# Letting a stage's row gathers be paced by free ring slots alone, without their wait for streamed dense tiles

## What is computed

```
def block(xb):                       # 128 tokens
    ...                              # top-k over product keys -> eidx, gate g
    u = u_tab[eidx]
    act = gelu(einsum('td,thkd->thk', xb, u))
    return einsum('thk,thkd->td', g * act, v_tab[eidx])
```

## Time and profile before

| | |
|---|---|
| median of 3 runs | 2384.32 us (2382.76 to 2390.59) |
| the profiled execution | 2381.75 us, of which the trace spans 2379.9 us |
| PE busy in the span | 2116.2 us |
| DVE busy | 1310.4 us |
| POOL busy | 892.9 us |
| data moved by DMA | 590.03 MB |
| gathers (queue q0) | 402.70 MB, 44.4% of 16 engines' span |

### The profile page before, as it was taken

How to read it: one execution, slowest core, us unless ns; L and a number is a source line. 1 busy time by engine, 2 the same in 40 slices (tenths; PEclk the granted TensorE clock), 3 DMA queues, 4 the chain that set the end, 5 groups by cost and what they waited for, 6 DMA issues and landing times.

```text
span 2379.9 us, 31321 instructions
## 1 busy us (share of the span) xinstructions
PE 2116.2 (89%) x12505; PEld 1569.1 (66%) x12505; DVE 1310.4 (55%) x2926; ACT 642.7 (27%) x1077; POOL 892.9 (38%) x821
## 2 busy tenths in 40 slices
PE   8999999999999998999999887889898887875775
PEld 8776879889887875888888654577785444311111
DVE  5855476776456466659798765689663233100000
ACT  4345332322454333331111143521111443100000
POOL 0500000000000000004577566557677665666664
PEclk9999999999999998999999998899999898897998
DMA  5111254444212210227999998989999998999997
GB/s 199 54 36 71 89 186 177 177 177 160 92 69 106 71 54 18 89 84 276 356 417 417 387 339 329 331 310 418 419 418 418 370 346 321 368 378 370 358 381 279
DMA packets 147057, 590.03 MB, mean 248 GB/s; under 512 B 16336, under 2 KB 16464, under 8 KB 134240
## 3 DMA queue, kind: packets, MB, share of 16 engines
q0 software_dynamic: 110592, 402.70, 44.4%
q1 hardware_dynamic: 35136, 178.80, 19.8%
q10 hardware_dynamic: 1184, 6.53, 0.7%
HBM read 584.29 MB, written 3.67 MB: 247 GB/s over the span
## 4 chain that ended last, share of the span: by engine, by line
PE 30%; DVE 13%; POOL 8%; issue 7%; DMA 6%; another core or an unknown queue 4%; ACT 3%; DVEq 0%; POOLq 0%; ACTq 0%
PE ps L1166 8%; DVE cols L1996 6%; POOL big L2687 5%; PE ps L1116 5%; PE ps L561 4%; PE ps L562 4%; PE ps L563 4%; DMA big<-vtab,big 2%; DMA big<-utab,cols 2%; PE ps L1103 2%; POOL hres L2687 2%; ACT Ir L2546 1%; PE ps L1130 1%; ACT Ir L2548 1%
## 5 line engine op out<-in xcount | busy, mean ns | idle before, releaser
L1103 PE MATMUL ps<-rowb,raw 128*128 128x256 f32 x2048 | 458.4, 384 | 23.6 <-DMA raw<-ucols 18.3
L1103 PEld LDWEIGHTS ps<-rowb,raw 128*128 128x128 f32 x2048 | 388.2, 192 | 90.5 <-issue 22.2
L1166 PE MATMUL ps<-big,cols 128*32 128x512 f32 x1392 | 362.7, 674 | 55.0 <-issue 32.0
L2687 POOL DMA_INDIRECT big<-vtab,big x348 | 338.6, 973 | 188.9 <-issue 84.0
L2611 POOL TENSOR_TENSOR small<-small,cols 128x1 f32<-128x1 f32 (+3 forms) x33 | 28.7, 872 | 886.1 <-DVE small L1612 387.4
L1166 PEld LDWEIGHTS ps<-big,cols 128*32 128x32 f32 x1392 | 70.4, 118 | 235.3 <-issue 149.2
L2687 POOL DMA_INDIRECT big<-utab,cols x139 | 177.7, 1278 | 86.3 <-issue 34.7
L1996 DVE CUSTOM_DVE_ANT_0 cols<-big 128x1024 bf16<-128x1024 f32 x139 | 167.9, 1226 | 40.4 <-DMA big<-utab,cols 27.5
L1116 PE MATMUL ps<-Aj,Ir 128*128 128x64 f32 x1024 | 159.0, 296 | 32.4 <-issue 23.9
L1166 PE MATMUL ps<-hres,cols 128*32 128x512 f32 x392 | 170.0, 666 | 18.8 <-issue 12.4
L2049 DVE TENSOR_TENSOR cols<-cols,ps 128x512 f32<-128x512 f32 x64 | 43.9, 688 | 246.3 <-PE ps L1116 138.8
(11 more groups left out here) (390 smaller groups left out, 4502.1 us busy)
## 6 DMA issues: line engine op xcount, KB each, us to landing
raw<-ucols SPq DMA_DIRECT2D x128, 512.0 KB
raw<-ff SPq DMA_DIRECT2D x32, 1024.0 KB, 5.0
raw<-w SPq DMA_DIRECT2D x24, 1024.0 KB, 4.8
raw<-ada SPq DMA_DIRECT2D x24, 1024.0 KB, 4.8
raw<-wo SPq DMA_DIRECT2D x8, 1024.0 KB, 4.8
raw<-wq SPq DMA_DIRECT2D x8, 1024.0 KB, 4.8
big<-vtab,big POOLq DMA_INDIRECT x348
hres<-x SPq DMA_DIRECT2D x8, 512.0 KB, 6.0
```

Of the source, the lines that this page charges most:

```text
L1103: ins = e.matmul(PS[b][:, c:c + 256], lhsT=un[j % NU][:, k, :], rhs=h2T[k // 4][:, k % 4, :], start=(k == 0), stop=(k == 7))
L1166: ins = e.matmul(PS[hf][32 * j:32 * j + 32, :], lhsT=win[:, c0:c0 + 32], rhs=gs[i][:, hf * 512:(hf + 1) * 512], start=(m == 0), stop=(m == ...
L2687: e.indirect_dma_start(gs[i], None, utab if st == "U" else vtab, bass.IndirectOffsetOnAxis(ap=idx, axis=0)).then_inc(sems[f"l_g{i}"], 16)
```

## The change

POOL's wait for the dense tiles in U1 is removed, and the constant with it. Nothing else changes: the same instructions, the same order on every engine, the same slots.

```
-BEHIND = 8
...
                     if st == "U":
                         G.wait_ge(*at[decoded(t, k)])
-                        if t and k >= BEHIND:
-                            for what, a, z in pace("U", t, k - BEHIND):
-                                if what == "dense" and z > a:
-                                    G.wait_ge(*at["dn", z - 1])
                         gather(st, t, k, eid[:, t, k:k + 1])
```

## The result

The changed kernel took 2422.88 us (median of 4 runs, 2399.24 to 2442.62), the kernel before 2383.54 us (4 runs, 2377.14 to 2390.59). The ratio is 1.0132, with a 95% interval of 1.0097 to 1.0168. The profiled execution took 2424.70 us, 42.95 more than that of before. Lines of the changed kernel stand two lower: gathers L2685, dots L1994, tiles' matmuls L1101, SP's tile loads L2742. ("L" numbers of experiments can be off by a few again.)

The account below looks back on a forecast made before the run. Full DMA engines at 418 GB/s were taken to bound U1. The profiled 2381.75 us, + 0 for tiles, - 0 for gathers, plus 2.57 us to the median, rounded to 2384 us; range of 8 in 10: 2375 to 2396 us.

Parts of the forecast that it names:

- U1 is as long as its bytes: In U1 the DMA engines are full, so its bytes set its length: 96.5 MB, 231 us at 418 GB/s.
- the sum of 184 pieces: U1's transfers from 1575 us: 122 gathers, 60 tile loads, write-out and read-back, 96.5 MB, through by 1806 us.
- The stall moves from `dn` to `dot`: In U1 POOL would wait for DVE's dots to free slots instead of PE's tiles; value 0.
- about 32 us in flight: A U1 gather's time in flight would grow from 19.34 us, with POOL up to 17 gathers ahead of DVE.
- The tiles lose nothing further; price 0: U1's tile loads would not slow when more gathers are queued; 0 us added.
- an even split: SP's tile queue and POOL's gather queue share bandwidth equally: 213 GB/s for tiles, which need 148.
- the far bound of +35: Upper cost from U1's beginning: 0.80 us of PE's wait per tile over 52 tiles, 42 us, less 7.
- U0, which I chose for its length: U0's 140 us without the wait, tiles 3.73 us each against 3.60 in U1: +1 us, taken as 0.
- Rival (b): Gathers crowd out U1's tile loads, which then finish last: +14, 2398 us; chance 0.16, spread from +7 to +35.
- (a): Rival: POOL's waits make U1's gathers late, so removal gains at most 7.02 us, 2377 us; over 0.3% faster has 0.09.
- (c): Rival: SP's write-out round trip in U1 takes longer behind more gathers, up to +3 us; no chance of its own.

Follow-up runs that it names:

- e7: The changed kernel as it is, run again where the kernel before took 2284.43 us; 2284.47 us, ratio 0.9996.
- e6: The changed kernel with POOL, from U1's gather 10 on, waiting for DVE's dot k - 10; 2383.51 us, 0.9997 of the kernel before.
- e13: The kernel before with its wait for the tiles loosened from step k - 8 to k - 16; 2385.71 us, ratio 1.0017.
- e14: The changed kernel with POOL at most 13 gathers ahead of DVE's dots in U1; 2381.18 us, 0.9992 of the kernel before.
- kind B: Groups of runs in which the kernel before takes about 2384 us, as in the recorded pair.
- kind A: Groups of runs in which the kernel before takes about 2284 us.
- e5: The changed kernel as it is, run again where the kernel before took 2385.18 us; 2395.39 us, ratio 1.0036.
- e11: The changed kernel as it is, run again where the kernel before took 2383.38 us; 2393.61 us, ratio 1.0033.
- e12: The changed kernel with SP's write-out of block 0 and read-back moved behind the last tile; 2379.18 us, 0.9982 of the kernel before.
- e1: The changed kernel with POOL at most 10 gathers ahead of DVE's dots in U1; 2285.83 us, 1.0001 of the kernel before.
- e10: The kernel before with its wait for the tiles loosened from step k - 8 to k - 16; 2284.27 us, ratio 1.0001.
- e15: The changed kernel with a small POOL power, in a new buffer, behind every second gather of U1; 2312.10 us, 1.0120 of the kernel before.
- e17: The changed kernel with a small POOL power, in a new buffer, behind every third gather of U1; 2301.91 us, 1.0080 of the kernel before.
- e18: The changed kernel with a small POOL power, in a new buffer, behind every fourth gather of U1; 2301.12 us, 1.0072 of the kernel before.

## Why the prediction was wrong, step by step

**"U1 is as long as its bytes"**: right, as long as gathers last. e7 took away all of POOL's waits for tiles and gained nothing (0.9996); with late marks absent, U1 kept 418 or 419 GB/s. In the changed kernel's recorded execution the rate holds too, until 1810 us, when the gathers have run out; from there the sum of 184 pieces no longer gives the time.

**"The stall moves from `dn` to `dot`", "about 32 us in flight"**: right. POOL waits for L1994 and no longer for PE; e7's gather was 31.25 us in flight. (17 gathers at 1.78 us are 30, not 32; the nearness of 31.25 to both decides nothing.) In the recorded execution the wait is short because the tiles' trouble left the bandwidth to the gathers.

**"The tiles lose nothing further; price 0"**: this is the step that failed. Its stated reason, an even split that does not depend on the other queue's length, held: 6.5 us from a tile load's issue to its landing with up to 13 gathers in flight, 6.7 in e7 with 14 to 16. What I had assumed without a row was the link ahead of it, that PE finishes a landed tile and its mark moves SP at once. In the recorded execution eight loads were issued 5.7 to 34.7 us late, and the term put at 0 came out at 43 us for the profiled launch. The profile of before had a trace of it that I did not look for: its load of tile 68 is issued 4.1 us after the end of tile 65, right behind POOL's free burst at U1's start, and I put the 2.57 us that PE then waited down to bandwidth. I even used them for the far bound of +35. If the rate of POOL's issues is what matters, which the count suggests and nothing shows, that stretch was the nearest thing to the changed kernel, and not U0, which I chose for its length.

**Rival (b)**: its picture came true, its mechanism did not. Named signs were a wait for `ucols` of 30 us or more (33.3), tile 123 behind the last dot (1857.5 against 1784.5) and a window well under 418 GB/s (163). But no tile load was crowded out. Its price, +14 with a far bound of +35, fell short of the +39 between the medians (+43 between the profiled executions), since I spread a small delay over 52 tiles, where most of it fell on eight.

**Why nothing stopped it** is my reading of the windows, argued and not tried by itself: with the gate, POOL waits for the same late tile, and the tiles find their bandwidth later with gathers still beside them. Without it the gathers go on at 420 GB/s, get up to 73 us ahead (1857.5 - 1784.5), and what is left at the end is tiles alone, one for each 3.45 us of PE's time, at 163 GB/s. The byte sum then no longer holds: half of the engines' time in those 47 us is lost. e6 (a cap of 10 to the dots, 0.9997) and e13 (`BEHIND = 16`, 1.0017) showed no runaway in 20 runs; e14 did in 2 of 11. At that frequency ten runs without one prove little for any single variant.

**(a)** did not happen anywhere: no variant's ratio is below 1 by more than its interval. **(c)** is small: from the write-out's issue to the read-back it is 8.66 us in the recorded execution, 8.66 in e7 and 8.59 before.

**What stays open.** Why marks of PE move SP and ACT late, and PE's matmuls come singly, in kind B only, and whether PE works late there or finished marks are held up. Small doses stand in every profile of kind B; why they become a runaway in some executions is open too. That it goes with gathers issued back to back is a count over eight profiles, not an experiment; the experiments meant for it met kind A, without the fault. Why the recorded four runs are so much slower (1.0132) than the fifteen of e5 and e11 (1.0036, 1.0033) is open as well; both hold long executions of the same sort (up to 2414.89), only fewer. No version was clearly faster than the kernel before: e12, the changed kernel with its write-out moved, comes closest in kind B (0.9982 [0.9963, 1.0001]) and is 0.9992 and 0.9999 in kind A.

## What to carry to other kernels

A wait that costs nothing because the bandwidth is full may still keep two streams in step; before it goes, ask what each does when the other is held up for 10 us, and whether work of one kind alone can fill the machine at the end. When an engine waits for a transfer, look at when that transfer was issued and at what its issuer waited for, before blaming the bandwidth. A change that takes out such a tie wants many executions and more than one chip: here it read 1.0132, 1.0036, 1.0033 and 0.9996. And when an experiment brings a buffer or an instruction of its own, look at the stages that it should not touch before naming its price.

## What the runs showed of the hardware

- The same kernel takes 2284 us in some groups of runs and 2384 us in others; V1 to V3 run at 418 to 420 GB/s in the former (e1 to e10) and at some 330 to 380 GB/s in the latter (339, 361 and 365 by stage in the recorded execution), while the changed kernel's U1 has 417 to 420 in both as long as gathers last.
- In the latter a mark of PE can move the engines that wait for it up to 34.7 us after the profile's end of its tile, both at the same time to 0.01 us, and PE's matmuls then start singly, some 1.4 to 2.1 us apart in the recorded execution.
- How many gathers must be in flight in such a mix: with 4 to 8 nearly all of the time (before, 94% of it) U1 had 418 or 419 GB/s, and with up to 16 (e7) no more than that. With mostly 3 or 4 (e15) it had 388 to 398, where the ceiling of that kernel was 409 in other stages.
- A 512 KB tile load beside queued gathers landed in a median of 6.5 to 6.7 us, whether at most 10, at most 13 or 14 to 16 of them were in flight; with none in flight it took 3.4 to 3.7 us (recorded execution, from 1816 us on).
- Three kernels with 68 more columns of buffer and a fill (e15, e17, e18) ran at no more than 410 GB/s in every stage, where the others in kind A reached 418 to 420. The cause was not tried.
